# The first norm's scale and bias of two token tiles: from VectorE to GpSimd, in a two-layer hybrid decoder step with a mixture of experts

## The reference, cut to what matters

```python
mix = jnp.concatenate([y_ssd, y_rg, y_ret], -1) @ w_out
x = _layernorm(ALPHA * x + (1.0 + g1) * mix, ln1_g, ln1_b)     # xhat * g + b
h2 = x * (1.0 + sc2) + sh2
scores = sigmoid(h2 @ router_w)        # router: two experts of the best of 4 groups
moe = sum over the token's two experts of w_e * (silu(h2 @ gate_e) * (h2 @ up_e)) @ down_e
x = _layernorm(ALPHA * x + (1.0 + g2) * moe, ln2_g, ln2_b)
```

## Time and profile before

| | |
|---|---|
| median of 3 runs | 1876.62 us (1869.5 to 1877.93) |
| the profiled execution, its own time | 1879.24 us |
| its span in the trace | 1877.4 us |
| PE busy | 1545.1 us, 82% |
| DVE busy | 744.8 us, 40% |
| ACT busy | 346.8 us, 18% |
| POOL busy | 116.8 us, 6% |
| DMA, mean over the span | 302 GB/s |

### The profile page before, as it was taken

One profiled execution on the slowest core, in us unless ns is written; L12 is line 12 of the kernel. 1 busy time (PEld: TensorE's weight loads), 2 busy tenths in 40 slices (PEclk: granted clock), 3 DMA queues, 4 the chain that ended last, 5 costly groups with the idle time before them and its releaser, 6 DMA issues.

```text
span 1877.4 us, 29665 instructions
## 1 busy us (share of the span) xinstructions
PE 1545.1 (82%) x11834; PEld 849.0 (45%) x11834; DVE 744.8 (40%) x1706; ACT 346.8 (18%) x787; POOL 116.8 (6%) x168
## 2 busy tenths in 40 slices
PE   5999999998867776677889999999976677666795
PEld 2764543545433333334366555354543334333442
DVE  0253565767312221222535266585732222122226
ACT  0235321203101111010223532120210111011001
POOL 4000002200200000000020000211000000000000
PEclk8899999988978888888989899998988889888877
DMA  9453447557999999999954543746789999999993
GB/s 321 152 191 139 124 127 209 167 198 293 380 405 427 428 428 428 428 429 428 401 210 164 200 124 101 224 127 227 285 347 427 428 428 428 428 427 428 429 426 129
DMA packets 94567, 567.56 MB, mean 302 GB/s; under 512 B 8245, under 2 KB 9021, under 8 KB 69138
## 3 DMA queue, kind: packets, MB, share of 16 engines
q1 hardware_dynamic: 82578, 532.05, 70.2%
q0 software_dynamic: 11904, 34.34, 6.5%
HBM read 550.55 MB, written 15.81 MB: 302 GB/s over the span
## 4 chain that ended last, share of the span: by engine, by line
PE 52%; DMA 38%; DVE 5%; issue 2%; SPq 1%; DVEq 1%; ACT 1%; ACTq 0%
DMA ring<-in_exp_w_up 35%; PE ps L1550 10%; PE ps L1017 9%; PE ps L992 9%; PE ps L1387 3%; PE ps L1239 3%; DMA ring<-in_w_ada 3%; PE ps L856 2%; PE ps L999 2%; PE ps L1208 1%; PE ps L1143 1%; PE ps L1184 1%; PE ps L1373 1%; PE ps L1567 1%; SPq L623 1%
## 5 line engine op out<-in xcount | busy, mean ns | idle before, releaser
L1550 PE MATMUL ps<-ring,xTb 128*32 128x256 f32 x4224 | 332.2, 484 | 232.8 <-DMA ring<-in_exp_w_up 220.6
L1550 PEld LDWEIGHTS ps<-ring,xTb 128*32 128x32 f32 x4224 | 164.7, 138 | 400.2 <-issue 357.8
L2745 DVE TENSOR_TENSOR hb<-sg,ps 128x128 f32<-128x128 f32 x66 | 25.0, 379 | 475.4 <-ACT sg L1932 475.4
L1017 PE MATMUL ps<-ring,hT 128*128 128x512 f32 x384 | 171.4, 599 | 0.0
L992 PE MATMUL ps<-hT,ring 128*128 128x288 f32 x640 | 165.0, 417 | 4.7 <-DVE hT L2089 2.5
L1523 PE MATMUL ps<-sel,h_tm 128*128 128x128 f32 (+1 forms) x912 | 162.9, 306 | 0.0
L1523 PEld LDWEIGHTS ps<-sel,h_tm 128*128 128x128 f32 x912 | 124.4, 188 | 52.8 <-issue 22.6
L992 PEld LDWEIGHTS ps<-hT,ring 128*128 128x128 f32 x640 | 122.7, 194 | 42.6 <-issue 8.4
L1932 ACT ACTIVATE sg<-ps 128x128 f32<-128x128 f32 x66 | 18.3, 277 | 605.1 <-PE ps L1550 605.1
L1567 PE MATMUL ps<-ring,hTb 128*32 128x256 f32 x2048 | 126.7, 389 | 2.5 <-DVEq L2748 2.5
L2753 DVE COPY ys<-ps 32x256 f32<-32x256 f32 x124 | 52.6, 424 | 161.1 <-PE ps L1567 159.9
(11 more groups left out here) (503 smaller groups left out, 1687.7 us busy)
## 6 DMA issues: line engine op xcount, KB each, us to landing
ring<-in_exp_w_gate SPq DMA_DIRECT2D x66, 2048.0 KB, 18.7
ring<-in_exp_w_up SPq DMA_DIRECT2D x66, 2048.0 KB, 23.2
ring<-in_exp_w_down SPq DMA_DIRECT2D x64, 2048.0 KB, 24.8
ring<-in_w_ada SPq DMA_DIRECT2D x24, 2048.0 KB, 10.2
ring<-in_w_in SPq DMA_DIRECT2D x22, 2048.0 KB, 9.1
ring<-in_w_out SPq DMA_DIRECT2D x8, 2048.0 KB, 9.1
h0s<-in_state_ssd POOLq DMA_DIRECT2D x16, 512.0 KB, 7.2
out_ssd_s<-h0s POOLq DMA_DIRECT2D x16, 512.0 KB, 5.3
```

The lines of the kernel that those rows point to most:

```text
L1017: last = mm(o[:, :], hT[:, k, T0[i]:T0[i] + P], w[:, k, :], start=(k == 0), stop=(k == KT - 1))
L1550: last = mm(ps[32 * j:32 * j + 32, b, 0:2 * P], xTb[:, k, m * BLK:(m + 1) * BLK], w[:, 0:2, k * D_EXPERT + j * P:k * D_EXPERT + (j + 1) * ...
```

## The change

The four scale and bias instructions of tiles 1 and 2 leave DVE's program and stand in POOL's. POOL starts them when the logits are complete (bank `logit` filled) and `lnp` has landed, then signals `x1_done`. DVE waits for `x1_done` only before the tail blocks, after the seven quads of experts.

```diff
@@ block.gpsimd
                 pool.dma_start(lnp[:, 1, :], A["ln1_b"][l]...).then_inc(ln1_in.sem, 16)
+                pool.wait_ge(filled.sem, fills(l, ("logit",)))
+                idle["pool"].stand(pool)
+                pool.wait_ge(ln1_in.sem, ln1_in.at(l, 32))
+                idle["pool"].stand(pool)
+                for n_ in range(2):
+                    for i in (1, 2):
+                        x_ = x_tm[0:ROWS[i], i, :]
+                        pool.tensor_tensor(x_, x_, lnp[0:ROWS[i], n_, :], (ALU.mult, ALU.add)[n_])
+                    pool.drain()
+                pool.drain().then_inc(x1_done.sem, 1)
                 pool.wait_ge(early_used.sem, early_used.at(l, 1))
@@ block.vector
                 select(QS, 0)
 
-                for n_ in range(2):
-                    for i in (1, 2):
-                        x_ = x_tm[0:ROWS[i], i, :]
-                        tt(x_, x_, lnp[0:ROWS[i], n_, :], (ALU.mult, ALU.add)[n_])
-                    D()
-                dve.sem_inc(x1_done.sem, 1)
 
                 cpy(nblk[:, 0, :], bank(("rank",))[:, 96:128]).then_inc(TD, 1)
@@
                 with dve.Fori(1, QUADS) as Q:
                     quad(Q, False)
 
+                dve.wait_ge(x1_done.sem, x1_done.at(l, 1))
+                idle["dve"].stand(dve)
                 tail = dve.value_load(npi[0:1, 0:1], min_val=2, max_val=TAILMAX)
```

## The result

The changed kernel takes 1883.78 us in the median of 13 runs (1878.89 to 1890.9), the kernel before 1876.62. The medians differ by 7.2 us. The ratio of times measured side by side is 1.0044 with a 95% interval of 1.003 to 1.0058, or about 8 us slower (6 to 11): just inside the 0.5% that I had called no change, and clear of 1 on the slow side. The profiled execution took 1888.97 us with a span of 1887.2.

What follows compares the result with a forecast made beforehand. Expert weight loads, started by the end of the first gate and up product, bound the kernel. Two layers of 8.9 us later gather less 12.4 us gained gave +5.4 us: forecast 1882 us, 8-in-10 range 1863 to 1891.

Steps and rivals of the forecast that it cites:

- The likeliest case: In the routing, POOL's four instructions each hold DVE about 2 us; 1882 us, chance 0.45.
- What bounds the kernel: Expert weight loads; their stream begins when PE ends the first gate and up product, so time there moves the program.
- DVE is relieved: Behind the selection, dbc copies end before the gather; the product starts 4.0 and 3.9 us earlier, with its clock kept.
- The length p: One POOL instruction of 1024 elements: 1.94 us, taken as two streams; bounds 0.97 and 2.91.
- The hold D: DVE's delay in the routing before the selection, from four POOL instructions: 6.6 us, bounds 2.7 and 10.4.
- PE's gaps: PE stands still before the rank product, weight rows or gather; the lowered clock costs 2.3 us.
- G: Time by which the gather starts later in each layer: 8.9 us, from 2.7 to 13.4.
- The sum: Over both layers, later gathers less the 12.4 us gained: +5.4 us, bounds -7.0 and +14.4.
- rival A: In the routing, POOL reads without holding DVE, so the full 12.4 us are gained: 1864 us; chance 0.22.
- Rival B: In the routing, POOL instructions nearer 2.9 us and the full clock price: +14.4 us, 1891; chance 0.28.
- Rival C: In layer 0, a late early load stands ahead of expert 2's loads, up to 4.9 us lost: about 1884; chance 0.05.
- the reload: POOL's reload in layer 0 delays its work by 0 to 20 us; costed at nothing.

Runs made afterwards that it cites:

- the half version: The changed kernel with only the samples' (tile 2's) two instructions on POOL, tile 1's two back on DVE behind the selection; 1874.13 us, ratio 0.9998.
- e9: The kernel before, nothing on POOL, with DVE's weight-row copies directly behind the selection, ahead of scale, bias and plan; 1870.69 us, ratio 0.9962.
- e2: The changed kernel with POOL's four reading instructions replaced by five clearings that only write; 1870.02 us, ratio 0.9966.
- e1: The changed kernel with POOL's four instructions left out, waits and signals kept; 1869.33 us, ratio 0.9957.
- e4: The changed kernel with POOL's start put off until DVE has made the selection; 1882.29 us, ratio 1.0032.
- e7: The kernel before with the samples' two instructions and tile 1's multiplication on POOL, begun ahead of the routing; 1875.72 us, ratio 0.9996.
- e3: The changed kernel with PE's filler ahead of the rank product seven times as long; 1885.26 us, ratio 1.0039.
- e10: e9 with two filler matmuls of PE in the pause between gather and first product; 1866.54 us, ratio 0.9949.
- e8: e7 with two filler matmuls of PE in the pause between gather and first product; 1875.51 us, ratio 0.9993.

## Why the prediction was right

The likeliest case came out, at the predicted place and by the predicted mechanism. That the number is so near owes something to luck, as two of the steps say. Step by step:

- *What bounds the kernel*: right. In the table, runs that move the end of the first product move the time, by amounts that agree within the intervals for all but two (the fillers in the kernel before gained 5 to 11 where the trace says 4.7; the half version, -4 to +3 where the trace says +3.1).
- *DVE is relieved*: right. The `dbc` copies are no longer what PE waits for, and e9 reproduces the gain with no work taken off DVE at all.
- *The length p*: 1.94 us taken, 2.35 measured (2.339 to 2.427), inside the bounds. The estimate from the Trainium skill's "GPSIMD Engine Reference", section "Elementwise — side-by-side cycle accounting", 2.25, was nearer than my two streams.
- *The hold D*: 6.6 taken, 7.65 and 7.6 measured. The mechanism is shown by the rows of the changed kernel together with e2 (writing holds nothing) and e1 (without the work, no hold). Missed: that POOL's drain opens a gap of 2 us between the pairs, which lengthens POOL's work but lets DVE run; and that one-input instructions can be held too (e4, e7).
- *PE's gaps*: 2.3 us taken, 1.6 and 2.1 measured (the gather starts 9.2 and 9.7 us later, less 7.65 and 7.6). G was 8.9 by the sum.
- *The sum*: +5.4 against +6.7 in the trace and about +8 in the runs. Its terms were off in both directions: by p alone (four holds in each of two layers, 0.4 us more each) the sum is 3.2 us too low, by what DVE got done meanwhile (1.8 and 1.7 us a layer instead of 1.2) 1.1 too high, and by PE's gaps 0.9 too high. That they nearly cancel is luck.
- *The 12.4 us of rival A*: mis-sized. 4.5 of them were the clock of the product, which I had put down to the stand of 4.8 us and counted as won. A pause of 0.87 us can lower it as well: it did in layer 1 of e1, both layers of e2 and e9 and layer 1 of e3. So relieving DVE alone is worth 9.0 us by the traces where both products came out slow (e2, e9) and 12.1 where both were fast (e10), and 6 to 8 in the medians of e1, e2 and e9. In the changed kernel's profiled execution both products ran at the full clock behind the same pause, which the prediction had no ground to count on: with both slow, some 3.3 us more would have been lost there (2 x (5.3 - 3.66)). Whether its other executions had them fast isn't known.
- *Rival B*: its price, +14.4, rested on the upper bound of p; the measured p lies just below the 2.4 from which it would have decided.
- *Rival C and the reload*: the early load is issued at 452.54, well in time, and DVE's new wait comes some 400 us behind POOL's work (the first row behind it, L2810, starts at 876.8). The reload cost nothing to be seen: its two rows, named `MODIFY_POOL_CONFIG` in the trace, last 11 ns each, and POOL's first instruction starts 0.36 us after the last logit matmul in layer 0 and 0.29 in layer 1.

## What to carry to other kernels

An instruction moved to POOL isn't hidden by being beside DVE's work. Each of these, which read two operands from SBUF, cost DVE its own length, less what DVE got done meanwhile in instructions that were not held (reductions, for one): on this chain of small dependent instructions 7.65 us of POOL's 9.42. Before moving work to another engine, look at what the waiting engine really waits for behind it: here the four instructions and the plan only stood in front of 1.2 us of copies, and putting the copies first gained about what moving the work had lost. And work out a gain that rests on the TensorE clock at both its levels: behind a pause of 0.87 us the product took up to 5.35 us, behind one of 4.61 it took 5.20.

## What the runs showed of the hardware that I had not expected

- POOL's reads held a DVE `TENSOR_SCALAR` with one input in SBUF (2.36 us instead of 0.18 in e4, 4.09 instead of 1.21 in e7), not only instructions with two. Reductions, and a `MEMSET` (0.14 us at 434.92 in e7, inside POOL's third instruction), ran on.
- POOL's 32-row instruction takes as long, and holds as long, as its 128-row one: 2.33 against 2.35 us.
- Behind a pause of 0.87 us the granted clock fell to 0.50 in six layers (e1, e2, e3, e9) and stayed whole in five (the changed kernel, e1, e7); no run here shows what decides it. With the pause filled it stayed whole in all four layers profiled (e8, e10), but in e7, without a filler, it did so too: only e10 against e9 speaks for the filler.
- Stretches that no edit touches vary from one profiled execution to the next: from the issue of expert 2's gate in layer 0 to PE's first turn in layer 1 it is 857.2 us before, 861.0 after, and 855.6 to 864.4 over all runs. Such differences, 3.7 us here, are why the spans of before and after differ by 9.8 us while the stretches that changed differ by 6.3.
